# Old-state contributions of three groups placed inside the weight unit that stood ahead of them

## The chip, the cores and the metric

The kernel runs on one core of one Trainium2 chip. The metric is the device time in microseconds (us) of one execution; lower is better. Engines are named as in the profile: PE (TensorE), with PEld for its weight loads, DVE (VectorE), ACT (ScalarE), POOL (GpSimd) and SP (SyncE).

## The reference

One layer of a streaming encoder on 512 prompt rows and 8 streams of 16 sampled rows, in fp32. Between two half-step feed-forward blocks stands a mixer with a gated linear recurrence (branch A) and a state-space branch (branch B). The change lies in branch B, in how the sampled rows use the state that they start from:

```python
x = x + 0.5 * _swiglu(_rmsnorm(x), ffn1)
proj = _rmsnorm(x) @ w_in               # lru_x | lru_gate | z | xBC | dt | gate logits
xbc  = silu(causal_conv(xbc))           # xs, B, C; four groups of eight heads
states = concat([h0, chunk states])     # h0: the old state of each stream
y_off  = einsum('bclgn,bcgepn,bcgel->bclgep', C, states_in, exp(A_cs))
y = y_diag + y_off + D * xs;  final state is an output too
m = g_lru * (y_lru @ w_br_lru) + g_ssd * (rmsnorm(y * silu(z)) @ w_br_ssd)
x = x + m @ w_out
x = x + 0.5 * _swiglu(_rmsnorm(x), ffn2)
```

For the sampled rows `states_in` is `h0`, so their part of `y_off` is C times the old state: the "contributions" below.

## The kernel before

Features lie on the 128 partitions and the 640 tokens (512 + 128) along the rows. Every weight matrix is taken in units of 1024 x 128 numbers (8 tiles of 128 x 128). SP loads a unit into `w_raw`, ACT rounds it to `w_hi` (L977), DVE subtracts to get `w_lo` (L1343), and PE multiplies, for each of 8 tiles k, `w_hi` and `w_lo` with `act_hi` and `w_hi` with `act_lo`, each in two halves of 320 tokens: 48 matmuls (L635), summed in a PSUM buffer. There are two such buffers, `pu0` and `pu1`, used in turn by all "outs": each unit's result, and also the results of `old_states` and `new_states` below. PE opens an out only when DVE has freed the one two before it (`out_free`, in `open_out`). ACT begins the weight cut for the unit after next when a unit's result is ready (`take`).

The order of the work is written out by hand, the same on each engine. Branch B goes through four groups g; in each, after five steps of the chunked scan, the sampled streams' part is done on PE in this order: a unit, `old_states(0)` (16 transposes of the first half of the old states, L879; DVE copies them to `h0_t`, L1786), `inner` (L840), the units named in `middle`, `from_states(0)` (16 contributions `h0_t` x C, 128 x 16 each, L889, into `pn0`; the profile has two matmul records and two weight loads for each), `old_states(1)`, `new_states(0)` (L901), `from_states(1)`, `new_states(1)`, and then the next units. `h0_t` holds one half of the old states only.

`middle` holds one unit in groups 0, 1 and 2 (one of the next group's B and C columns, "xb") and none in group 3. What the others do with its result sets when its PSUM buffer is free: ACT takes its cut (L977), copies the result to `ext` (L1079 to L1082), DVE does three convolution taps (L1337) and frees the buffer after the first. DVE's own order there is: sums of squares (L1358), the three taps, then the copies of `old_states(1)` (L1786). ACT squares (L988) just ahead of the cut. `xf`, `es`, `h0_a` and `h0_b` are rows, decays and old states of the group (the profile writes `h_t`, `h_a`, `h_b`).

Of the kernel before, what the change touches and what calls it, by code (L numbers as in the profile page):

```python
# [17 lines left out]
P = 128  # L18
D_MODEL = 1024
SEQ, DEC_B, DEC_L = 512, 8, 16  # L20
TOK = SEQ + DEC_B * DEC_L
HALF = TOK // 2
KT = D_MODEL // P
# [72 lines left out]
U_AT, O_AT = {}, {}  # L96
# [67 lines left out]
def layer(nc, x_prompt, x_sample, state_lru_conv, state_lru_h, state_ssd_conv, state_ssd_h,  # L164
# [7 lines left out]
    with ctx:  # L172
        def sb(stack, name, shape, dt=F32):
            return stack.enter_context(nc.sbuf_tensor(name, shape, dt))

        s = {n: ctx.enter_context(nc.semaphore(n)) for n in SEMAPHORES}
# [8 lines left out]
        act_hi = sb(ctx, "act_hi", [P, KT, TOK], F32R)  # L185
        act_lo = sb(ctx, "act_lo", [P, KT, TOK], F32R)
# [81 lines left out]
        with ExitStack() as sc:  # L268
# [12 lines left out]
            h0_t = sb(sc, "h0_t", [P, 2, DEC_B, NS])  # L281
# [7 lines left out]
        pn = [ctx.enter_context(nc.psum_tensor(f"pn{i}", [P, 2, 512], F32)) for i in range(2)]  # L289
# [9 lines left out]
        def xft(g, k):  # L299

            return xf[:, k, :] if k < PAIRS else bc[:, g % 2, k - PAIRS, :]
# [10 lines left out]
        def out(o):  # L312

            return pu[o % 2][:, :, 0:HALF]
# [19 lines left out]
        def _(sp):  # L334
# [14 lines left out]
            def load_ffn(u, o, ci, w_up, w_down, first):  # L349
                tile0 = 0  # L350
                for gi, n, uu, _, _, ud, _ in ffn_plan(u, o, ci):
                    with sp.Fori(1 if first and gi == 0 else 0, n) as i:
                        for k in range(2):
                            load(k, uu, 2, i, cols(w_up, i * P + (tile0 * P + k * FFN)))
                    with sp.Fori(0, KT // 2) as i:
                        for k in range(2):
                            load(k, ud, 2, i, cols(w_down, i * (2 * P) + k * P, tile0, n), n)
                    tile0 += n
# [260 lines left out]
        def _(pe):  # L619
            def open_out(o):  # L620

                if not (isinstance(o, int) and o < 2):
                    pe.wait_ge(s["out_free"], o - 1)

            def products(dst, side, tiles, hi, lo, ready=None):

                n, at, ins = 3 * len(tiles), 0, None
                for k, c in tiles:  # L630
                    for w, a in ((w_hi, hi), (w_lo, hi), (w_hi, lo)):
                        if ready and w is w_hi and k >= ready[3]:
                            pe.wait_ge(s[ready[0 if a is hi else 1]], ready[2] + (k + 1))
                        for h in range(2):
                            ins = pe.matmul(dst[:, h, :], w[:, side, c, :], a[:, k, h * HALF:(h + 1) * HALF],  # L635
                                            start=(at == 0), stop=(at == n - 1))
                        at += 1
                ins.then_inc(s["out_ready"], 1)

            def unit(ub, ob, per_u, per_o, i, hi, lo, nk=KT, ready=None):  # L640

                pe.wait_ge(s["w_lo_done"], i * per_u + (ub + 1))
                open_out(i * per_o + ob)
                products(out(ob), ub % 2, [(t, t) for t in range(nk)], hi, lo, ready)

            def norm_sum(sq_end):

# [68 lines left out]
            for t in range(NT):  # L716
                pe.wait_ge(s[f"xin{t}"], 16)
                open_out(t)
                for k in range(KT):
                    ins = pe.transpose(pu[t % 2][:, k // 4, (k % 4) * P:(k % 4 + 1) * P],  # L720
                                       x_rows[:, t, k * P:(k + 1) * P], ident[:, :])
# [23 lines left out]
            for t in range(NT):  # L745
                ins = pe.transpose(pn[1][:, 0, t * HEADS:(t + 1) * HEADS], dt_raw[:, t * P:(t + 1) * P], ident[0:HEADS, 0:HEADS])
# [8 lines left out]
            for t in range(NT):  # L755
                pe.matmul(pn[1][:, 0, t * HEADS:(t + 1) * HEADS], gt_mask[:, t // (NT - 1), :], da_col[:, t, :],
                          start=True, stop=True)
            for t in range(NT):
                pe.matmul(pn[1][:, 1, (NT + t) * HEADS:(NT + t + 1) * HEADS], le_mask[:, t // (NT - 1), :], da_col[:, t, :],
                          start=True, stop=True)  # L760
            pe.matmul(pn[1][:, 1, 0:(NT - 1) * HEADS], ones[:, :],
                      da_col[:, 0:NT - 1, :].rearrange("p t h -> p (t h)"),
                      start=True, stop=True).then_inc(s["dt_p"], 1)
# [5 lines left out]
            for t in range(NT):  # L769
                ins = pe.transpose(pn[0][0:HEADS, t // 4, (t % 4) * P:(t % 4 + 1) * P], e_col[:, t, :], ident[:, :])  # L770
# [4 lines left out]
            with pe.Fori(4, KT) as j:  # L775
                lru_pair(j)

            def mix_unit(name, hi, lo, ready=None):
                unit(U_AT[name], O_AT[name], 0, 0, 0, hi, lo, ready=ready)

            def branch_unit(g, r):

                u, o = U_AT["br", g, r], O_AT["br", g, r]
                pe.wait_ge(s["w_lo_done"], u + 1)
                for m in range(2):
                    open_out(o + m)
                    products(out(o + m), u % 2, [(k, 2 * k + m) for k in range(PAIRS)], yn_hi, yn_lo,
                             ready=("yn_hi_done", "yn_lo_done", g * PAIRS, 0) if r == 0 and m == 0 else None)

            def lru_branch_unit(m):  # L790
                mix_unit(("bl", m), yl_hi, yl_lo, ("yl_hi_done", "yl_lo_done", 0, 0) if m == 0 else None)

            def fill(names):
                for name in names:
                    if name[0] == "br":
                        branch_unit(*name[1:])
                    elif name[0] == "bl":
                        lru_branch_unit(*name[1:])
                    else:
                        mix_unit(name, act_hi, act_lo)  # L800

            fill([("gl", 0), ("xb", 0, 4), ("xb", 0, 5)])
            for g in range(GROUPS):
# [31 lines left out]
                def inner(t):  # L835

                    sv(t, SV_G)
                    for h in range(HPG):
                        r = HD * (h % 2)
                        ins = pe.matmul(pn[0][r:r + HD, 0, (h // 2) * P:(h // 2 + 1) * P], xd[:, h, :], lmat[:, h, :],  # L840
                                        start=True, stop=True)
                    ins.then_inc(s["ssd_p"], 1)

                before, beside, behind, sampled_unit, middle, after = FILL[g]
                for k in range(PAIRS):
                    mix_unit(("xb", g, k), act_hi, act_lo)
                    if g and k == NORM_AT - 1:
                        norm_sum(SQ_GRP + g * SQG)
                fill(before)

                for t in range(NT - 1):
# [5 lines left out]
                    for q in range(PAIRS):  # L857
                        ins = pe.matmul(pn[0][:, 1, q * P:(q + 1) * P],  # L858
                                        ht[:, 2 * q:2 * q + 2, :].rearrange("n a b -> n (a b)"),
                                        xft(g, 5)[:, t * P:(t + 1) * P], start=True, stop=True)  # L860
                    ins.then_inc(s["ssd_p"], 1)
                    pe.matmul(pn[1][:, 1, :], b_tok[:, :], xdd[:, :, :].rearrange("p h d -> p (h d)"),  # L862
                              start=True, stop=True).then_inc(s["ssd_p"], 1)
# [3 lines left out]
                for q in range(PAIRS):  # L867
                    ins = pe.transpose(pn[1][:, 1, q * P:(q + 1) * P],
                                       ht[:, 2 * q:2 * q + 2, :].rearrange("n a b -> n (a b)"), ident[:, :])
                ins.then_inc(s["hp_mm"], 1)  # L870

                def old_states(qq):

                    pe.wait_ge(s[f"h0_in{qq}"], g * 32 + 32)
                    for a in range(2):
                        o = O_AT["old", g, qq] + a
                        open_out(o)
                        for b in range(DEC_B):
                            ins = pe.transpose(pu[o % 2][:, b // 4, (b % 4) * P:(b % 4 + 1) * P], h0[qq][:, a, b, :], ident[:, :])  # L879
                        ins.then_inc(s["out_ready"], 1)  # L880

                def from_states(qq):

                    for a in range(2):
                        q = 2 * qq + a
                        pe.wait_ge(s["out_free"], O_AT["old", g, qq] + a + 1)
                        for b in range(DEC_B):
                            c = SEQ + b * DEC_L
                            ins = pe.matmul(pn[0][:, 1, q * P + b * DEC_L:q * P + (b + 1) * DEC_L], h0_t[:, a, b, :],  # L889
                                            xft(g, 5)[:, c:c + DEC_L], start=True, stop=True)  # L890
                    return ins

                def new_states(qq):

# [12 lines left out]
                fill(sampled_unit)  # L907
                old_states(0)
                inner(NT - 1)
                fill(middle)  # L910
                from_states(0)
                old_states(1)
                pe.wait_ge(s["bseq"], g + 1)
                new_states(0)
# [13 lines left out]
            for a in range(TAIL_OUTS):  # L928
# [3 lines left out]
                for b in range(8):  # L932
                    ins = pe.transpose(pn[a % 2][0:rows, b // 4, (b % 4) * P:(b % 4 + 1) * P],
                                       src[:, 8 * (a % 4) + b, :], ident[:, :])
                ins.then_inc(s["tail_mm"], 1)
            with pe.Fori(0, KT // 2) as i:
                for k in range(2):
                    unit(U_OUT + k, O_OUT + k, 2, 2, i, act_hi, act_lo,
                         ready=("mh_done", "ml_done", 0, 0) if k == 0 else None)
            ffn(U_FFN2, O_FFN2, 22, h_hi, h_lo, act_hi, act_lo, XH_FFN2, last_sum, lambda: None)  # L940

            def to_rows(t, k):
                return pe.matmul(fin_at[t][:, k // 4, (k % 4) * P:(k % 4 + 1) * P], resid[:, k, t * P:(t + 1) * P], g_fin[:, k, :],
                                 start=True, stop=True)
# [9 lines left out]
            for k in range(KT):  # L954
                ins = to_rows(2, k)
            ins.then_inc(s["out_ready"], 1)
            pe.wait_ge(s["sq_added"], SQ_FIN + KT)
            for t in range(NT):
                ins = pe.matmul(pn[0][:, 0, t:t + 1], rvar[:, t * P:(t + 1) * P], ones[:, 0:1], start=True, stop=True)
            ins.then_inc(s["sq_summed"], 1)  # L960
            pe.wait_ge(s["y_a"], 1)
            for k in range(KT):
                ins = to_rows(3, k)
            ins.then_inc(s["out_ready"], 1)
            pe.wait_ge(s["y_v"], 1)
            for k in range(KT):
                ins = to_rows(4, k)
# [982 lines left out]
```

## Time and profile before

| | |
|---|---|
| median of 3 runs | 1974.1 us (1973.32 to 1975.79) |
| profiled execution | 1978.57 us |
| its span | 1977.0 us |
| PE busy | 1918.2 us, 97% of the span |
| DVE busy | 1078.0 us, 55% |
| ACT busy | 725.0 us, 37% |
| mean granted PE clock | 0.974 of full |

The span runs from the first to the last instruction that the profiler saw; the execution's own time is a little more. A busy PE isn't PE at its peak: matmuls are pipelined, and its clock has two levels, full (2.4 GHz) and half (1.2 GHz). The "granted clock" of a stretch is the mean over it, 1.00 at full and 0.50 at half.

### The profile page before, as it was taken

To read this page: it belongs to the slowest core of one execution; us is meant where nothing else is said; L and a number is where in the kernel's file an instruction comes from. 1 tells how busy PE (TensorE), PEld (TensorE's weight loads), DVE (VectorE), ACT (ScalarE), POOL (GpSimd) and SP (SyncE) were. 2 spreads that over 40 slices of the span, in tenths; PEclk is the share of its full clock that TensorE was granted. 3 is DMA by queue.
4 is the path that set the end of the run, shared out by engine and by line. 5 is a ranking of instruction groups with operands and counts; after the bars stand their busy time and mean duration, and the time that the engine had idled before them with its cause. 6 is when DMAs were issued, how large, how long until landed. Compare 5 with 4: busy or idle time off the path is not lost.

```text
span 1977.0 us, 31917 instructions
## 1 busy us (share of the span) xinstructions
PE 1918.2 (97%) x12877; PEld 1859.4 (94%) x12877; DVE 1078.0 (55%) x1355; ACT 725.0 (37%) x1141; POOL 113.0 (6%) x219
## 2 busy tenths in 40 slices
PE   8999999998899999999999999998799999999998
PEld 7999999998799999989998998987799999999998
DVE  6442443345687654566577677666745433442444
ACT  5221332223477644334545444542333221221222
POOL 2000000000012100001011010100000000000000
PEclk9999999999899999999998998997899999999999
DMA  4222222222222242334224323322622222222222
GB/s 140 74 70 75 68 83 73 76 67 84 91 72 74 72 119 86 95 98 124 78 70 113 103 78 111 96 69 78 224 76 65 74 75 76 74 76 76 75 66 77
DMA packets 268066, 171.68 MB, mean 87 GB/s; under 512 B 6534, under 2 KB 259642, under 8 KB 267677
## 3 DMA queue, kind: packets, MB, share of 16 engines
q1 hardware_dynamic: 239840, 129.52, 22.8%
q0 software_dynamic: 7072, 26.34, 4.3%
q10 hardware_dynamic: 21072, 14.69, 2.3%
q8 instruction: 57, 0.93, 0.2%
q14 instruction: 25, 0.20, 0.0%
HBM read 150.03 MB, written 20.48 MB: 86 GB/s over the span
## 4 chain that ended last, share of the span: by engine, by line
PE 85%; DVE 7%; ACT 3%; issue 2%; DMA 1%; DVEq 0%; ACTq 0%
PE pu L635 76%; PE pu L901 1%; DMA merged<-gate_spill 1%; PE pn L830 1%; PE pn L889 1%; ACT w_hi L977 1%; PE pn L858 1%; PE pn L840 1%; DVE h_t L1786 1%; PE pn L862 1%; DVE w_lo L1343 1%; DVE bc L1337 1%; DVE squares L1337 1%; PE pu L692 0%; DVE h_a L1793 0%
## 5 line engine op out<-in xcount | busy, mean ns | idle before, releaser
L1343 DVE TENSOR_TENSOR w_lo<-w_raw,w_hi 128x1024 fp32r<-128x1024 f32 x240 | 295.7, 1232 | 503.1 <-ACT w_hi L977 501.2
L635 PE MATMUL pu<-act_hi,w_hi 128*128 128x320 f32 x2336 | 542.3, 313 | 12.2 <-ACT act_hi L1004 7.4
L635 PE MATMUL pu<-act_lo,w_hi 128*128 128x320 f32 x2336 | 534.8, 310 | 2.1 <-DVE act_lo L1384 2.0
L635 PE MATMUL pu<-act_hi,w_lo 128*128 128x320 f32 x2336 | 534.0, 310 | 0.0
L977 ACT ACTIVATE w_hi<-w_raw 128x1024 fp32r<-128x1024 f32 x240 | 253.6, 1057 | 536.6 <-PE pu L635 532.9
L635 PEld LDWEIGHTS pu<-act_hi,w_hi 128*128 128x128 f32 x2336 | 394.4, 189 | 28.0 <-issue 21.0
L635 PEld LDWEIGHTS pu<-act_lo,w_hi 128*128 128x128 f32 x2336 | 391.9, 189 | 3.5 <-DVE act_lo L1384 3.1
L635 PEld LDWEIGHTS pu<-act_hi,w_lo 128*128 128x128 f32 x2336 | 392.8, 189 | 0.0
L635 PE MATMUL pu<-h_hi,w_hi 128*128 128x320 f32 x1056 | 241.7, 310 | 0.7 <-DVE ff_g L1401 0.7
L635 PE MATMUL pu<-h_lo,w_hi 128*128 128x320 f32 x1056 | 241.5, 310 | 0.0
L635 PE MATMUL pu<-h_hi,w_lo 128*128 128x320 f32 x1056 | 241.0, 309 | 0.0
L635 PEld LDWEIGHTS pu<-h_hi,w_hi 128*128 128x128 f32 x1056 | 177.4, 189 | 1.1 <-DVE ff_g L1401 0.9
L635 PEld LDWEIGHTS pu<-h_lo,w_hi 128*128 128x128 f32 x1056 | 177.4, 189 | 0.3 <-DVE h_lo L1410 0.3
L635 PEld LDWEIGHTS pu<-h_hi,w_lo 128*128 128x128 f32 x1056 | 177.3, 189 | 0.0
L635 PE MATMUL pu<-yn_hi,w_hi 128*128 128x320 f32 x256 | 63.7, 331 | 7.3 <-DVE acc_ssd L1663 5.3
L1012 ACT ACTIVATE ff_t<-ff_g 128x640 f32<-128x640 f32 x44 | 32.6, 740 | 92.5 <-DVE ff_g L1401 92.5
L635 PE MATMUL pu<-yn_lo,w_hi 128*128 128x320 f32 x256 | 59.8, 315 | 3.5 <-DVE yn_lo L1856 3.5
L1232 ACT ACTIVATE m_hi<-le_mask,da_hr 128x128 fp32r<-128x128 f32 x160 | 48.9, 390 | 29.5 <-PE pn L889 22.8
L635 PE MATMUL pu<-yn_hi,w_lo 128*128 128x320 f32 x256 | 59.3, 313 | 0.0
L635 PEld LDWEIGHTS pu<-yn_hi,w_hi 128*128 128x128 f32 x256 | 44.1, 193 | 12.8 <-DVE acc_ssd L1663 6.1
L1337 DVE SCALAR_TENSOR_TENSOR ff_a<-ff_t,ff_g 128x640 f32<-128x640 f32 x44 | 36.3, 826 | 35.4 <-ACT ff_t L1012 35.4
L1232 ACT ACTIVATE m_lo<-le_mask,da_lo 128x128 fp32r<-128x128 f32 x160 | 48.8, 388 | 0.0
(319 smaller groups left out, 1980.0 us busy)
## 6 DMA issues: line engine op xcount, KB each, us to landing
w_raw<-in_ffn_w_up_dram SPq DMA_DIRECT2D x87, 512.0 KB, 3.8
w_raw<-in_w_in_dram SPq DMA_DIRECT2D x73, 512.0 KB, 3.9
w_raw<-in_ffn_w_down_dram SPq DMA_DIRECT2D x32, 512.0 KB, 3.8
w_raw<-in_w_br_ssd_dram SPq DMA_DIRECT2D x16, 512.0 KB, 3.4
w_raw<-in_ffn_w_down_dram SPq DMA_DIRECT2D x16, 384.0 KB, 3.4
es<-e_spill POOLq DMA_DIRECT2D x40, 128.0 KB, 2.9
merged<-gate_spill POOLq DMA_DIRECT2D x8, 640.0 KB, 5.3
h_a<-in_state_ssd_h_dram POOLq DMA_DIRECT2D x8, 512.0 KB, 6.3
```

What stands on the lines that cost most here:

```text
L635: ins = pe.matmul(dst[:, h, :], w[:, side, c, :], a[:, k, h * HALF:(h + 1) * HALF], start=(at == 0), stop=(at == n - 1))
L830: ins = pe.matmul(pn[1][:, b, :], gt_r[:, t // (NT - 1), :], m[:, 4 * b:4 * b + 4, :].rearrange("p h l -> p (h l)"), start=(part == 0), st ...
L840: ins = pe.matmul(pn[0][r:r + HD, 0, (h // 2) * P:(h // 2 + 1) * P], xd[:, h, :], lmat[:, h, :], start=True, stop=True)
L858: ins = pe.matmul(pn[0][:, 1, q * P:(q + 1) * P], ht[:, 2 * q:2 * q + 2, :].rearrange("n a b -> n (a b)"), xft(g, 5)[:, t * P:(t + 1) * P] ...
L862: pe.matmul(pn[1][:, 1, :], b_tok[:, :], xdd[:, :, :].rearrange("p h d -> p (h d)"), start=True, stop=True).then_inc(s["ssd_p"], 1)
L889: ins = pe.matmul(pn[0][:, 1, q * P + b * DEC_L:q * P + (b + 1) * DEC_L], h0_t[:, a, b, :], xft(g, 5)[:, c:c + DEC_L], start=True, stop=True)
L901: ins = pe.matmul(pu[o % 2][:, b, :], xdd[rows, 2 * q:2 * q + 2, :].rearrange("p h d -> p (h d)"), b_seq[rows, :, :].rearrange("p b n -> p ...
L977: act.activation(w_hi[:, side, :, :], w_raw[:, side, :, :], ACT.Copy).then_inc(s["w_hi_done"], 1)
L1012: act.activation(ff_t[:, :], ff_g[:, :], ACT.Tanh, scale=0.5).then_inc(s["ff_th"], 1)
L1232: ins = act.activation(dst[:, h, :], le_mask[:, t // (NT - 1), :], ACT.Copy, scale=col)
L1337: return dve.scalar_tensor_tensor(out=dst, in0=a, scalar=scalar, in1=b, op0=op0, op1=op1)
L1343: dve.tensor_tensor(w_lo[:, side, :, :], w_raw[:, side, :, :], w_hi[:, side, :, :].bitcast(F32), ALU.subtract).then_inc(s["w_lo_done"], 1)
```

## The change

In groups 0, 1 and 2 the middle unit takes functions to be called amid its tiles: after tile k = 2 the eight contributions of the first part of `from_states(0)`, after tile k = 5 those of the second part. Before, both followed the unit. Group 3 has no middle unit and keeps its order. No wait is added or dropped: each part waits for its copy (`out_free`) as before.

```diff
@@ -622,7 +622,7 @@
                 if not (isinstance(o, int) and o < 2):
                     pe.wait_ge(s["out_free"], o - 1)
 
-            def products(dst, side, tiles, hi, lo, ready=None):
+            def products(dst, side, tiles, hi, lo, ready=None, amid=None):
 
 
 
@@ -635,13 +635,15 @@
                             ins = pe.matmul(dst[:, h, :], w[:, side, c, :], a[:, k, h * HALF:(h + 1) * HALF],
                                             start=(at == 0), stop=(at == n - 1))
                         at += 1
+                    if amid and k in amid:
+                        amid[k]()
                 ins.then_inc(s["out_ready"], 1)
 
-            def unit(ub, ob, per_u, per_o, i, hi, lo, nk=KT, ready=None):
+            def unit(ub, ob, per_u, per_o, i, hi, lo, nk=KT, ready=None, amid=None):
 
                 pe.wait_ge(s["w_lo_done"], i * per_u + (ub + 1))
                 open_out(i * per_o + ob)
-                products(out(ob), ub % 2, [(t, t) for t in range(nk)], hi, lo, ready)
+                products(out(ob), ub % 2, [(t, t) for t in range(nk)], hi, lo, ready, amid)
 
             def norm_sum(sq_end):
 
@@ -775,8 +777,8 @@
             with pe.Fori(4, KT) as j:
                 lru_pair(j)
 
-            def mix_unit(name, hi, lo, ready=None):
-                unit(U_AT[name], O_AT[name], 0, 0, 0, hi, lo, ready=ready)
+            def mix_unit(name, hi, lo, ready=None, amid=None):
+                unit(U_AT[name], O_AT[name], 0, 0, 0, hi, lo, ready=ready, amid=amid)
 
             def branch_unit(g, r):
 
@@ -879,16 +881,20 @@
                             ins = pe.transpose(pu[o % 2][:, b // 4, (b % 4) * P:(b % 4 + 1) * P], h0[qq][:, a, b, :], ident[:, :])
                         ins.then_inc(s["out_ready"], 1)
 
+                def from_state(qq, a):
+
+                    q = 2 * qq + a
+                    pe.wait_ge(s["out_free"], O_AT["old", g, qq] + a + 1)
+                    for b in range(DEC_B):
+                        c = SEQ + b * DEC_L
+                        ins = pe.matmul(pn[0][:, 1, q * P + b * DEC_L:q * P + (b + 1) * DEC_L], h0_t[:, a, b, :],
+                                        xft(g, 5)[:, c:c + DEC_L], start=True, stop=True)
+                    return ins
+
                 def from_states(qq):
 
-                    for a in range(2):
-                        q = 2 * qq + a
-                        pe.wait_ge(s["out_free"], O_AT["old", g, qq] + a + 1)
-                        for b in range(DEC_B):
-                            c = SEQ + b * DEC_L
-                            ins = pe.matmul(pn[0][:, 1, q * P + b * DEC_L:q * P + (b + 1) * DEC_L], h0_t[:, a, b, :],
-                                            xft(g, 5)[:, c:c + DEC_L], start=True, stop=True)
-                    return ins
+                    from_state(qq, 0)
+                    return from_state(qq, 1)
 
                 def new_states(qq):
 
@@ -907,8 +913,10 @@
                 fill(sampled_unit)
                 old_states(0)
                 inner(NT - 1)
-                fill(middle)
-                from_states(0)
+                if middle:
+                    mix_unit(middle[0], act_hi, act_lo, amid={2: lambda: from_state(0, 0), 5: lambda: from_state(0, 1)})
+                else:
+                    from_states(0)
                 old_states(1)
                 pe.wait_ge(s["bseq"], g + 1)
                 new_states(0)
```

On PE, in group 0, inside the middle unit: the rows at the unit's third and fourth tile (`pu0` is the unit's PSUM buffer, `act_hi` and `act_lo` the two parts of the activations, `w_hi` and `w_lo` of the weights). Before:

```order
L635 MATMUL pu0<-act_hi,w_hi 128x320 x2
L635 MATMUL pu0<-act_hi,w_lo 128x320 x2
L635 MATMUL pu0<-act_lo,w_hi 128x320 x2
L635 MATMUL pu0<-act_hi,w_hi 128x320 x2
L635 MATMUL pu0<-act_hi,w_lo 128x320 x2
L635 MATMUL pu0<-act_lo,w_hi 128x320 x2
```

In the changed kernel the first eight contributions (`pn0<-bc,h0_t`) stand between the two tiles:

```order
L635 MATMUL pu0<-act_hi,w_hi 128x320 x2
L635 MATMUL pu0<-act_hi,w_lo 128x320 x2
L635 MATMUL pu0<-act_lo,w_hi 128x320 x2
L890 MATMUL pn0<-bc,h0_t 128x16 [waits out_free]
L890 MATMUL pn0<-bc,h0_t 128x16 x7
L635 MATMUL pu0<-act_hi,w_hi 128x320 x2
L635 MATMUL pu0<-act_hi,w_lo 128x320 x2
L635 MATMUL pu0<-act_lo,w_hi 128x320 x2
```

At the unit's end, on PE in the same group, the rows from the last tile to the transposes of the second half of the old states (`h0_b`). Before:

```order
L635 MATMUL pu0<-act_hi,w_hi 128x320 x2
L635 MATMUL pu0<-act_hi,w_lo 128x320 x2
L635 MATMUL pu0<-act_lo,w_hi 128x320 x2
L889 MATMUL pn0<-bc,h0_t 128x16 [waits out_free]
L889 MATMUL pn0<-bc,h0_t 128x16 x7
L889 MATMUL pn0<-bc,h0_t 128x16 [waits out_free]
L889 MATMUL pn0<-bc,h0_t 128x16 x7
L879 MATMUL pu1<-ident,h0_b 128x128 [waits out_free,h0_in1]
L879 MATMUL pu1<-ident,h0_b 128x128 x7
L879 MATMUL pu0<-ident,h0_b 128x128 [waits out_free]
L879 MATMUL pu0<-ident,h0_b 128x128 x7
```

In the changed kernel:

```order
L635 MATMUL pu0<-act_hi,w_hi 128x320 x2
L635 MATMUL pu0<-act_hi,w_lo 128x320 x2
L635 MATMUL pu0<-act_lo,w_hi 128x320 x2
L881 MATMUL pu1<-ident,h0_b 128x128 [waits out_free,h0_in1]
L881 MATMUL pu1<-ident,h0_b 128x128 x7
L881 MATMUL pu0<-ident,h0_b 128x128 [waits out_free]
L881 MATMUL pu0<-ident,h0_b 128x128 x7
```

The transposes follow the unit's last matmul directly; what waits for what is the same as before, and the other engines' orders are unchanged.

## Rows read from the trace of the kernel before

**Rows 1.** The page: busy time of each engine, its share of the span, instructions.
```profile
PE 1918.2 (97%) x12877; PEld 1859.4 (94%) x12877; DVE 1078.0 (55%) x1355; ACT 725.0 (37%) x1141; POOL 113.0 (6%) x219
```

**Rows 2.** Timeline of group 0: start and length in us, engine, line, operation, [idle before].
```profile
830.25 2.17 PE L879 MATMUL pu<-ident,h_a 128*128 128x128 f32 x16
...
830.58 1.06 ACT L977 ACTIVATE w_hi<-w_raw 128x1024 fp32r<-128x1024 f32 x1 [4.56 <-PE pu L635]
...
832.81 2.35 DVE L1786 COPY h_t<-pu 128x1024 f32<-128x1024 f32 x2
...
834.18 0.53 PE L635 MATMUL pu<-act_hi,w_hi 128*128 128x320 f32 x2 [0.74 <-DVE h_t L1786]
...
840.55 2.94 DVE L1358 TENSOR_TENSOR rvar<-rvar,squares 128x512 f32<-128x512 f32 x4
...
841.30 3.64 PE L889 MATMUL pn<-bc,h_t 128*128 128x16 f32 x32
841.34 1.36 ACT L988 ACTIVATE squares<-xf 128x512 f32<-128x512 f32 x2 [2.04 <-DVE rvar L1358]
842.60 1.04 ACT L977 ACTIVATE w_hi<-w_raw 128x1024 fp32r<-128x1024 f32 x1
...
846.26 1.57 PEld L879 LDWEIGHTS pu<-ident,h_b 128*128 128x128 f32 x8 [0.32 <-DVE bc L1337]
847.96 2.35 DVE L1786 COPY h_t<-pu 128x1024 f32<-128x1024 f32 x2
...
849.33 2.17 PE L901 MATMUL pu<-b_seq,xdd 64*128 64x512 f32 x8 [1.10 <-DVE h_t L1786]
...
851.42 3.74 PE L889 MATMUL pn<-bc,h_t 128*128 128x16 f32 x32
...
855.10 3.47 PE L901 MATMUL pu<-b_seq,xdd 64*128 64x512 f32 x8
...
858.50 0.72 PE L635 MATMUL pu<-act_hi,w_hi 128*128 128x320 f32 x2
```

**Rows 3.** PE in stretches: bounds, length, busy time (instructions), granted clock, DMA share, GB/s.
```profile
834.18:841.30 7.12, 7.12 (x49) 1.00 0.26 72
...
844.78:848.25 3.47, 3.45 (x18) 0.56 0.61 149
...
1033.51:1037.58 4.07, 4.07 (x35) 0.85 0.00 0
...
1041.53:1044.26 2.73, 2.73 (x9) 0.70 0.02 6
1044.26:1049.08 4.82, 4.82 (x34) 0.74 0.69 200
1049.08:1052.80 3.72, 3.72 (x10) 0.50 0.09 25
1192.71:1196.20 3.49, 3.49 (x35) 1.00 0.00 0
...
1200.74:1204.07 3.33, 3.33 (x9) 0.57 0.00 0
1204.07:1208.33 4.26, 4.26 (x34) 0.85 0.75 220
1208.33:1212.05 3.72, 3.72 (x10) 0.50 0.11 30
...
1344.44:1351.23 6.79, 3.66 (x18) 0.50 0.00 0
1351.23:1354.94 3.71, 3.71 (x8) 0.50 0.02 4
1354.94:1361.88 6.94, 6.94 (x34) 0.50 0.51 151
1361.88:1365.60 3.72, 3.72 (x10) 0.50 0.00 0
```

**Rows 4.** The transposes of the old states (L879) of the second half, on PE: minimum, median, maximum ns.
```profile
L879 PE MATMUL pu<-ident,h_b x64: 272/421/476, 844.8 to 1347.7; 128*128 128x128 f32 x64
```

## The prediction

> **What bounds the kernel now.** I read the page first: TensorE (PE) is busy for 1918.2 us, 97% of the span, VectorE (DVE) for 55% [rows 1]. So time is lost only where PE waits, or where it runs at the lower of its two clock levels. The change touches one place, three times: the end of each of groups 0, 1 and 2. I then read the timeline of that place in group 0 [rows 2]; groups 1 and 2 repeat its pattern. Last I cut the same place of all four groups into stretches by what PE does, and read the granted clock of each [rows 3].
>
> What the reader is to see in group 0: The middle weight unit (L635) starts on PE at 834.18. At 841.30 PE goes on to the first 16 old-state contributions ("pieces" from here on: 32 short matmul records, L889), and at 844.78 to the transposes of the second half of the old states (L879). While the pieces run, the others deal with the unit's result: ScalarE (ACT) starts its weight cut at 842.60, then copies the result out, and DVE convolves it. Only when DVE's first tap has freed that PSUM buffer may PE do the second eight transposes (their weight loads start at 846.26). Then DVE finishes the taps, copies the transposed states (847.96), and only this copy lets PE start the new states (L901, 849.33). So from the unit's end to 849.33 the end is set by ACT and DVE, not by PE: the 3.48 us of pieces are work that PE does for nothing, under cover of a wait.
>
> **The change part by part.** Nothing is added or removed: 16 contributions (32 matmul records) in each of three groups move from behind the unit into it, eight behind its third tile and eight behind its sixth. There are no new semaphore increments and no DMA. Neither piece of eight waits: both copies that they need are DVE's 2.35 us from 832.81, over by 835.16 [rows 2], and the first piece would start three eighths into a unit of 7.12 us, 834.18 + 2.67 = 836.85. Switching between the forms costs nothing that I can see in a row; I take 0 (at most some 0.1 us a joint, two new joints a group, 0.6 us in all).
>
> What the move does is to make the unit end 3.48 us later, while the chain ACT cut, copy out, taps, state copy starts only at the unit's end. Before, the cut started 842.60 − 841.30 = 1.30 us behind the unit, since ACT was busy with squares until 842.70. At another unit, where ACT was idle, it started 830.58 − 830.25 = 0.33 us behind. So the later chain gets 0.97 us back and starts 3.48 + 0.33 − 1.30 = 2.51 us later than before [rows 2]. From the cut to the start of the new states it takes 849.33 − 842.60 = 6.73 us, none of it PE's own speed as long as the second transposes (start 846.26, 3.66 us behind the cut) end before the taps do.
>
> Now the new length of the place, counted from where the unit ends in the kernel before to where PE starts the next dense unit:
> 3.48 (pieces, now inside the unit) + 0.33 + 6.73 + first new states + second pieces + last new states.
> The last three depend on PE's clock, and here the rows give both levels. First new states: 851.42 − 849.33 = 2.09 at full clock, 3.71 in group 3 at half. Second pieces: 855.10 − 851.42 = 3.68 at full, 6.94 in group 3 at half. Last new states: 3.72 at half (groups 1 to 3), 2.09 at full [rows 2, 3]. So a group takes 18.40 us all at full clock and 24.91 us all at half.
>
> Before, it took 858.50 − 841.30 = 17.20, 1052.80 − 1033.51 = 19.29 and 1212.05 − 1192.71 = 19.34 us: 55.83 in the three [rows 2, 3].
>
> Which clock? The granted clock fell to half (1.2 GHz) behind every run of pieces in the kernel before: 0.56 in the transposes behind those of group 0, 0.85 already within those of group 1 [rows 3]. It came back to full (2.4 GHz) at once where PE then had full work, and late where it didn't: group 3, which has no middle unit, did its transposes and then idled (3.66 us busy in 6.79), and the clock stayed at 0.50 through 3.71, 6.94 and 3.72 us. Now look at what PE has after the change. Pieces of half the length between tiles of dense matmuls will probably no longer pull the clock down by themselves. But behind the unit there are then 0.33 + 6.73 = 7.06 us before the new states, with 16 transposes in them and else waiting. Group 0 needs 3.47 us for such 16 with most of the clock at half; at full each takes 272 ns instead of 421 [rows 4], so they are over sooner still. That is as little work as in group 3's stretch (3.66 us in 6.79). So I expect the clock to fall in that wait, after which the first new states run at half (3.71), the last ones too (3.72), and the second pieces lie between the rows of groups 1 and 2 (4.82, 4.26: the clock came back during the first new states and was lost again) and group 3's 6.94. I take the middle of 4.54 and 6.94, 5.74. A group: 3.48 + 7.06 + 3.71 + 5.74 + 3.72 = 23.71; three: 71.1; against 55.83: **+15.3 us**.
>
> The Trainium skill, page "TensorE: Matmul & The Clock Gate", section "Loop structure matters more than you think", speaks against this change in the same sense: matmuls that follow each other immediately stay warm, and a wait between bursts sends the array to half rate. Taken to its end, half rate from the wait onward, it gives the all-half case, which is the second rival below; group 3's 0.50 rows agree with it, the 1.00 of group 0's second pieces shows that short waits don't do it.
>
> Group 3 itself is not edited, but it will meet the clock in another phase of its work. Its second pieces ran wholly at half (6.94); in two of three other cases they cost about 4.5. It can hardly get worse: −2.4 × 2/3 = −1.6 us. Nothing else moves; the waits of PE behind this place are on DVE and ACT, which come as late as PE, so nothing swallows the delay. Sum: 15.3 − 1.6 = **+13.7 us**. The profiled execution took 1978.57 us (span 1977.0), 4.5 above the median of the runs shown, 1974.1; the sum is a difference, and I add it to the median: 1987.8.
>
> **The rivals.**
> 1. *The clock behaves as in group 0 now* (falls only for the last new states, 3.40 us there): 3.48 + 7.06 + 2.09 + 3.68 + 3.40 = 19.71 a group, 59.1 in all, +3.3 us, 1977.4. For it: two windows of full clock in group 0 in spite of a short wait. Against: the wait is now 5 us in two parts, not 1.1.
> 2. *All half*: 24.91 a group, +18.9 us, no help from group 3: 1993.0. If besides the pieces still pull the clock down within the unit, its last two tiles (a quarter of 7.12 us) may take twice as long, +1.8 us a group: 1998.
> 3. *The clock as in groups 1 and 2* (first new states 2.73 or 3.33, pieces 4.54, last 3.72): 21.83 a group, +9.7, 1983.8, or 1982 with group 3's gain. I count it with the forecast's own range.
> 4. *Faster, by the clock*: the short pieces hold the full level through the unit, and the waits are too short to lose it. Then 18.40 a group, 55.2 in three: −0.6 us, no change that can be told. It becomes faster only if group 3 also escapes: at full clock its two new-state blocks and pieces would save 1.62 + 3.26 + 1.63 = 6.5 us, in all −7: 1967. It decides only if the granted clock stays 1.00 through the waits of all four groups; the 0.50 of group 3 speaks against it.
> 5. *The move hides itself*: the unit's result was not urgent, because DVE is late anyway. Then +0: 1974. Against: the transposes waited for DVE's taps [rows 2], and DVE's sums of squares are over by 840.55 + 2.94 = 843.49 in either order.
>
> **How the numbers follow.** Chances: the forecast with case 3 (+8 to +17) 0.62; all half or worse 0.22; case 1 0.09; full clock or hidden, no change, 0.05; faster 0.02. What a measurement of this kernel can tell from no change is about 0.2%, 4 us. Case 1 lies just inside that, half of it goes to "same": slower 0.88, same 0.10, faster 0.02. The likeliest is 1987.8. The range leaves out part of the worst case above and case 1 and better below: 1979 to 1995.
>
> **What the changed profile would show.** Right: in groups 0 to 2 the unit's L635 matmuls span some 10.6 us with two blocks of pieces in it; ACT's cut starts about 0.3 us behind it; PE idles some 2.9 us before the second eight transposes, then about 2 us before the new states; granted clock 0.50 from that wait on, and second pieces over 4.2 us. Wrong: granted clock 1.00 there, ACT's cut later than 0.3 us behind the unit, or a stretch from the unit's start to the next dense unit of less than 7.12 + 20 us (nearer 18.40 than 23.71 behind the unit). What would make the forecast wrong is the clock: all of the spread between +3 and +19 hangs on it.

## The result: slower by 0.7%

The changed kernel takes 1987.62 us (median of 6, 1986.66 to 1991.53), the kernel before 1974.94 (median of 6, 1971.3 to 1976.34). The ratio is 1.0068, with a 95% interval of 1.0047 to 1.0088. The profiled execution took 1991.53 us with a span of 1989.9, against 1978.57 and 1977.0. Both lie some 4 us above the median of their kernel, so in other executions single groups may have taken less than the profiles show.

The page of the changed kernel: busy time of each engine, as in [rows 1].

```profile
PE 1921.1 (97%) x12877; PEld 1859.9 (93%) x12877; DVE 1078.5 (54%) x1355; ACT 725.7 (36%) x1141; POOL 112.7 (6%) x219
```

PE's busy time grew by 2.9 us, with the same number of instructions, in a span longer by 12.9. Neither the page's totals nor its list of lines tells where; the place itself does. The timeline of group 0 in the changed kernel, which answers to [rows 2] (start and length in us, engine, line, operation, [idle before]; contributions are now L890, transposes L881, ACT's cut L985, taps L1345, copies L1794, new states L907):

```profile
833.87 0.53 PE L635 MATMUL pu<-act_hi,w_hi 128*128 128x320 f32 x2 [0.74 <-DVE h_t L1794]
...
836.59 1.85 PE L890 MATMUL pn<-bc,h_t 128*128 128x16 f32 x16
...
841.01 1.85 PE L890 MATMUL pn<-bc,h_t 128*128 128x16 f32 x16
841.03 1.36 ACT L996 ACTIVATE squares<-xf 128x512 f32<-128x512 f32 x2 [2.03 <-DVE rvar L1366]
...
844.55 1.04 PE L881 MATMUL pu<-ident,h_b 128*128 128x128 f32 x8
...
844.75 1.06 ACT L985 ACTIVATE w_hi<-w_raw 128x1024 fp32r<-128x1024 f32 x1 [2.36 <-PE pu L635]
...
847.49 2.73 DVE L1345 SCALAR_TENSOR_TENSOR bc<-ext,vec,bc 128x640 f32<-128x640 f32 x3 [0.35 <-ACT bc L1090]
848.42 0.85 PEld L881 LDWEIGHTS pu<-ident,h_b 128*128 128x128 f32 x8 [3.08 <-DVE bc L1345]
848.43 1.09 PE L881 MATMUL pu<-ident,h_b 128*128 128x128 f32 x8 [2.84 <-DVE bc L1345]
...
850.13 2.35 DVE L1794 COPY h_t<-pu 128x1024 f32<-128x1024 f32 x2
...
851.49 3.78 PE L907 MATMUL pu<-b_seq,xdd 64*128 64x512 f32 x8 [1.97 <-DVE h_t L1794]
```

ACT had done its squares at 842.39 and stood idle for 2.36 us, until the unit had ended (844.55). The cut starts 0.20 us behind the unit, but that is 3.76 us behind where the unit used to end (833.87 + 7.12 = 840.99), against 1.30 before. PE waits twice: its weight loads stand 3.08 us and its matmuls 2.84 us for DVE's first tap, where the weight loads of [rows 2] stood 0.32 us and the matmuls had no gap; then its matmuls stand 1.97 us for DVE's copy, where [rows 2] had 1.10.

PE in stretches, as in [rows 3] (bounds, length, busy time, granted clock, DMA share, GB/s): group 0 first, then group 1 from the transposes on, group 2, and group 3, which the change does not touch.

```profile
833.87:840.99 7.12, 7.12 (x52) 1.00 0.26 73
840.99:844.55 3.56, 3.56 (x31) 1.00 0.00 0
844.55:848.43 3.88, 1.04 (x11) 1.00 0.06 6
848.43:851.49 3.06, 1.09 (x8) 0.80 0.59 164
851.49:855.21 3.72, 3.72 (x9) 0.50 0.00 0
855.21:862.14 6.93, 6.93 (x34) 0.50 0.54 154
862.14:865.86 3.72, 3.72 (x10) 0.50 0.00 0
1044.94:1051.88 6.94, 3.00 (x19) 0.74 0.29 76
1051.88:1055.37 3.49, 3.49 (x8) 0.54 0.02 5
1055.37:1059.48 4.11, 4.11 (x34) 0.88 0.79 226
1059.48:1063.20 3.72, 3.72 (x10) 0.50 0.12 34
...
1214.31:1218.03 3.72, 3.72 (x9) 0.50 0.00 0
1218.03:1224.96 6.93, 6.93 (x34) 0.50 0.53 151
1224.96:1228.68 3.72, 3.72 (x10) 0.50 0.00 0
...
1372.56:1376.44 3.88, 3.88 (x34) 0.94 0.85 242
```

The clock is at full through the unit with its two blocks of contributions, in all three groups (10.68 us at 1.00 in groups 1 and 2 too). In group 0 it is still 1.00 through the first wait, 0.80 over the second transposes and the second wait, and 0.50 from the new states on. In groups 0 and 2 everything from the new states to the next dense unit runs at half. (A dense unit is a weight unit: 48 matmuls of 320 columns, one behind the other.)

### The profile page after: what moved, and what is told of

The parts are those of the page before. It is cut to its first block, busy times and chain, and to the rows that moved or that the text cites. A ratio compares the mean times of both kernels' runs of the same rounds, so it can differ in the third digit from the quotient of the medians.

```text
span 1989.9 us, 31917 instructions
## 1 busy us (share of the span) xinstructions
PE 1921.1 (97%) x12877; PEld 1859.9 (93%) x12877; DVE 1078.5 (54%) x1355; ACT 725.7 (36%) x1141; POOL 112.7 (6%) x219
## 4 chain that ended last, share of the span: by engine, by line
PE 87%; DVE 6%; ACT 3%; issue 2%; DMA 1%; DVEq 0%; ACTq 0%
PE pu L635 77%; PE pn L890 2%; PE pu L907 1%; PE pn L832 1%; DMA merged<-gate_spill 1%; PE pn L860 1%; PE pn L842 1%; ACT w_hi L985 1%; PE pn L864 1%; DVE w_lo L1351 1%; DVE bc L1345 1%; DVE h_t L1794 1%; DVE squares L1345 1%; DVE xc L1345 0%; PE pn L652 0%
## 5 line engine op out<-in xcount | busy, mean ns | idle before, releaser
L985 ACT ACTIVATE w_hi<-w_raw 128x1024 fp32r<-128x1024 f32 x240 | 253.7, 1057 | 544.5 <-PE pu L635 541.4
L1345 DVE SCALAR_TENSOR_TENSOR ff_a<-ff_t,ff_g 128x640 f32<-128x640 f32 x44 | 36.3, 826 | 35.5 <-ACT ff_t L1020 35.5
```

What stands on the lines that cost most here:

```text
L985: act.activation(w_hi[:, side, :, :], w_raw[:, side, :, :], ACT.Copy).then_inc(s["w_hi_done"], 1)
L1345: return dve.scalar_tensor_tensor(out=dst, in0=a, scalar=scalar, in1=b, op0=op0, op1=op1)
```

## The experiments

For each kernel I read two lengths in its profile, group by group, from the timeline of PE. Both count from the start of the middle unit plus 7.12 us, which is where the whole unit used to end (in group 3, from the start of its first contributions): to the start of the first new states, and to the start of the next dense unit. Kernels are named by what they do; all were timed beside the kernel before.

| kernel | median us (before) | ratio, 95% interval | to the new states, groups 0, 1, 2 | to the next unit, groups 0, 1, 2, 3 |
|---|---|---|---|---|
| before | 1974.94 | | 8.03, 8.02, 8.02 | 17.20, 19.29, 19.34, 25.17 |
| changed | 1987.62 (1974.94) | 1.0068, 1.0047 to 1.0088 | 10.50, 10.50, 10.50 | 24.87, 21.82, 24.87, 21.95 |
| half inside | 1983.0 (1974.08) | 1.0039, 1.0023 to 1.0055 | 8.73, 8.71, 8.72 | 23.10, 21.89, 20.03, 25.17 |
| early tiles | 1990.95 (1974.08) | 1.0085, 1.0069 to 1.0101 | 13.63, 15.21, 10.50 | 24.72, 26.45, 21.83, 25.17 |
| late cut | 1989.3 (1974.08) | 1.0078, 1.0061 to 1.0095 | 10.33, 10.33, 10.33 | 21.50, 24.70, 21.68, 23.98 |
| filled waits | 1979.56 (1974.08) | 1.0022, 1.0008 to 1.0036 | 10.50, 10.50, 10.50 | 19.60, 21.23, 19.59, 22.12 |
| spread first | 1975.24 (1974.44) | 0.9998, 0.9988 to 1.0008 | 8.03, 8.03, 8.02 | 18.46, 17.62, 17.95, 25.17 |
| spread both | 1968.89 (1974.44) | 0.9970, 0.9959 to 0.9980 | 8.03, 8.03, 8.02 | 16.61, 16.61, 16.62, 22.01 |
| spread all | 1963.53 (1974.44) | 0.9938, 0.9922 to 0.9954 | 8.02, 8.02, 8.02 | 16.60, 16.60, 16.60, 19.38 |
| second only | 1971.75 (1974.44) | 0.9986, 0.9975 to 0.9997 | 8.03, 8.02, 8.02 | 18.04, 17.14, 17.26, 25.98 |
| changed, clock kept | 1970.45 (1974.34) | 0.9978, 0.9967 to 0.9988 | 10.52, 10.51, 10.51 | 19.09, 19.09, 19.08, 19.38 |

Within a kernel the column for the new states agrees to 0.02 us, but for "early tiles", where the clock fell within the unit: it is the chain on ACT and DVE. The last column scatters for one and the same order of work, by up to 4.6 us between the groups of a kernel and by 3.2 us in group 3 where it is not edited: it is the clock. It is read from one execution of each kernel, the ratio from all of them.

**Half inside.** The second eight contributions stand behind the eighth and last tile, so the unit ends before them.

```diff
-amid={2: lambda: from_state(0, 0), 5: lambda: from_state(0, 1)}
+amid={2: lambda: from_state(0, 0), 7: lambda: from_state(0, 1)}
```

> Only the first eight contributions stay inside the middle unit (behind its third tile); the second eight follow its last matmul, as before. My theory (the unit's result comes later by the time of the pieces inside it, and DVE's state copies with it): the unit ends 1.8 us later instead of 3.6, the weight cut, held until 1.30 us behind the old end by squares, starts some 0.8 us later, the first new states too, and the place of three groups costs 2 to 9 us more than in the kernel before: about +5, 1980. Rival (what costs is the cutting up of the unit, by joints or by the clock inside it): half the joints, half the cost of the full change, +6.5, and the new states start no later than in the kernel before.

The new states start 8.72 us behind the unit's old end, 0.70 later than before. The unit had grown by 1.78 us, so 1.08 of them were free: ACT is at its squares in that time. The rival's "no later than before" is out. The time rose by 0.39%, some 8 us, within the 2 to 9 expected but above the 5 in the middle, and more than 3 × 0.7 us explain; the rest is half clock, from the first new states on in group 0 (3.71, 6.94 and 3.72 us).

**Early tiles.**

```diff
-amid={2: lambda: from_state(0, 0), 5: lambda: from_state(0, 1)}
+amid={0: lambda: from_state(0, 0), 1: lambda: from_state(0, 1)}
```

> Both parts inside the unit, but behind its first and second tile instead of the third and sixth. My theory: only the unit's end counts, which is the same, so the time is that of the changed kernel, +12.5 within 3 us. Rival (the places inside the unit matter, because two blocks close together pull the clock down within the unit): the last six tiles run partly at half clock, up to 3.4 us more a group, up to +23 in all.

The granted clock in the unit, from its start to behind the second block, and over its last six tiles, in groups 0, 1 and 2:

```profile
831.89:838.14 6.25, 6.25 (x44) 0.84 0.31 82
838.14:845.70 7.56, 7.56 (x37) 0.68 0.00 0
1031.47:1039.12 7.65, 7.65 (x44) 0.68 0.24 66
1039.12:1046.86 7.74, 7.74 (x37) 0.66 0.00 0
1197.58:1202.89 5.31, 5.31 (x44) 1.00 0.35 98
1202.89:1208.26 5.37, 5.37 (x39) 1.00 0.00 0
```

The rival's mechanism is there: two blocks only one tile apart pulled the clock down within the unit in two groups of three, and six tiles took 7.6 and 7.7 us instead of 5.37. What failed in my expectation is that the unit would end as in the changed kernel. That its end sets the new states holds: they start 6.94 us behind it in all three groups (852.64 − 845.70 in group 0), as in the changed kernel (851.49 − 844.55). The total is 16.9 us above the kernel before, just outside my 12.5 within 3, and far from the rival's 23; against the changed kernel it is about 3 us more, and the two intervals overlap. A later end of 3.1 us in group 0 cost nothing in all (24.72 us against 24.87), as the clock came back sooner behind it.

**Late cut.** The order on PE is that of the kernel before; ACT gets three copies, whose result nobody uses, ahead of the middle unit's cut (the line that adds the semaphore `pad` is left out).

```diff
+                if middle:
+                    act.wait_ge(s["xb_out"], XB_AT[middle[0]])
+                    for r in range(3):
+                        act.activation(rtmp[:, :], act_hi[:, r, :].bitcast(F32), ACT.Copy).then_inc(s["pad"], 1)
+                        act.wait_ge(s["pad"], 3 * g + r + 1)
                 fill(middle)
```

> The order of the kernel before on PE, contributions behind the unit; added are three copies of 640 columns on ACT (into a scratch row that is free) ahead of the middle unit's weight cut in groups 0 to 2, some 2.5 us, so that the cut starts as late against PE's work as in the changed kernel. My theory: PE loses the same as in the changed kernel without any edit of its own order, since the new states start 2.5 us later and the clock falls in the wait: +8 to +19, about +13. Rival (the move on PE costs by itself, the chain behind the unit has slack): within 3 us of the kernel before.

Its timeline in group 0:

```profile
839.35 3.64 PE L889 MATMUL pn<-bc,h_t 128*128 128x16 f32 x32
...
842.93 1.06 ACT L977 ACTIVATE w_hi<-w_raw 128x1024 fp32r<-128x1024 f32 x1
...
846.61 1.97 PE L879 MATMUL pu<-ident,h_b 128*128 128x128 f32 x8 [2.54 <-DVE bc L1342]
...
849.68 3.79 PE L901 MATMUL pu<-b_seq,xdd 64*128 64x512 f32 x8 [1.10 <-DVE h_t L1791]
```

The cut starts 3.58 us behind the unit, the new states 10.33. No matmul of PE stands elsewhere in its order, and the kernel loses 0.78%, as much as the change. This is the sharpest test of the chain: the delay of ACT's cut is enough, and the rival "the chain has slack" is out.

**Filled waits.** The changed kernel with dense matmuls whose result nobody uses in PE's two waits: 18 ahead of the second eight transposes, 12 ahead of the new states.

```diff
+                def dense(n):
+                    for _ in range(n):
+                        for h in range(2):
+                            pe.matmul(pn[1][:, h, 0:HALF], gt_r[:, 0, :], act_hi[:, 0, h * HALF:(h + 1) * HALF],
+                                      start=True, stop=True)
...
+                        if qq == 1 and a == 1 and middle:
+                            dense(9)
...
+                if middle:
+                    dense(6)
```

> The changed kernel with 18 matmuls of 320 columns (result unused) on PE ahead of the second eight transposes and 12 ahead of the new states, in groups 0 to 2, so that PE works through its two waits; the chain on ACT and DVE is as late as in the changed kernel. My theory: the waits stay as long, but the granted clock stays 1.00 there; the group takes about 18.4 us instead of 23.9, that is 12 to 17 us less than the changed kernel and within 4 us of the kernel before. Rival (the cost is the wait alone, the clock little): within 3 us of the changed kernel, +12.7.

Its timeline in group 0, from the new states on:

```profile
852.57 2.17 PE L916 MATMUL pu<-b_seq,xdd 64*128 64x512 f32 x8 [0.21 <-DVE h_t L1805]
...
854.67 3.75 PE L899 MATMUL pn<-bc,h_t 128*128 128x16 f32 x32
...
858.34 1.99 PE L916 MATMUL pu<-b_seq,xdd 64*128 64x512 f32 x8
...
860.30 2.35 DVE L1822 TENSOR_TENSOR h_b<-h_b,pu 128x1024 f32<-128x1024 f32 x2
...
861.67 0.53 PE L635 MATMUL pu<-act_hi,w_hi 128*128 128x320 f32 x2 [1.34 <-DVE h_b L1822]
```

The new states start as late as in the changed kernel, and now run at full clock (2.10 us instead of 3.72). The rival ("the clock little") is out, but that gave back 8 to 9 us, not 12 to 17; it stands at +0.22%. The last row says why: at full clock PE comes to the next unit 1.34 us too early. DVE adds to `h_b` only after its outputs, which wait for the contributions, and so frees the buffer late. Half clock had hidden that wait. In group 1 the clock fell in the contributions once more (0.73 over them, 0.50 over the last new states; 21.23 us).

**Spread first, spread both, spread all, second only.** From the kernel before; quarters of the first contributions are put between dense matmuls and transposes (first part), the second contributions in halves around one of the last new states, which DVE adds ahead of its outputs (second part). The edit is shown shortened: calls that stand one to a line in the kernel are joined, and the splitting of the helpers is left out.

```diff
-                from_states(0)
-                old_states(1)
+                from_state(0, 0, 0, 4); dense(3); from_state(0, 0, 4, 8); dense(2)
+                from_state(0, 1, 0, 4); old_state(1, 0); dense(1)
+                from_state(0, 1, 4, 8); old_state(1, 1); dense(1 if middle else 10)
...
                 new_states(0)
-                from_states(1).then_inc(s["ssd_p"], 1)
-                new_states(1)
+                from_state(1, 0); new_state(1, 0); dense(2)
+                from_state(1, 1).then_inc(s["ssd_p"], 1); new_state(1, 1)
...
-                outputs(NT - 1, lambda: new_states(1))
+                new_states(1, (0,))                       # on DVE
+                outputs(NT - 1, lambda: new_states(1, (1,)))
```

"Spread first" has the first part in groups 0 to 2, "spread both" both parts there, "spread all" both in all four groups, "second only" the second part in all four.

> Kernel before, unit whole, in groups 0 to 2: behind the unit the contributions go in quarters between dense matmuls (3 and 2 pairs of 320 columns whose result is unused) and between the two halves of the second transposes, all inside the wait that PE has there (new states not before 8.03 us behind the unit). Theory (the new states' start is set by ACT and DVE; the rest of a group's length is PE's clock): the new states start at 8.0 us in every group and run at full clock, 2.1 us instead of 2.7 and 3.3 in groups 1 and 2, the second contributions as before; a group takes 17.2 to 18.5 us, together 52 to 55 against 55.8: 0 to -4 us. Rival (PE's work behind the unit isn't covered, so that the added matmuls cost what they take): 3 x 1.8 us, +5.

> The last one, and behind the first new states the other contributions in two halves, with half of the last new states and 2 unused dense pairs between them; DVE adds that half ahead of its outputs, so that the next unit's buffer comes free earlier. Theory: the clock is kept to the end, and the next unit starts 16.5 us behind the middle unit's end: 49.5 us in three groups against 55.8, -6 us. Rival (what is gained behind the new states is lost again, since the contributions end 1.6 us later and ACT and DVE wait for them): 0 to -2 us.

> The same in group 3 too, which has no middle unit: there 10 unused dense pairs fill PE's wait for the state copies. Group 3's place took 25.2 us at half clock; theory at full: 10.8 to the new states + 2.1 + 1.84 + 1.05 + 0.6 + 1.84 + 1.05, 19.3 us: -6 more, -12 in all, 1962. Rival (the half clock of group 3 costs nothing, since DVE is the bound there): as the last one, -6.

> Only the second half of the last change, in all four groups (other contributions in two halves around half of the last new states, 2 unused dense pairs, DVE adds that half first); the first contributions whole behind the unit, as in the kernel before. Theory: the next unit no longer waits for DVE behind the contributions, and about half of the clock losses of the last new states (1.6 us each) go: -2 to -5 us. Rival (no clock gain without the first part, as the clock is already down): -1 to +2.

The timeline of "spread all" in group 0, from the second transposes on:

```profile
847.51 1.07 PE L890 MATMUL pu<-ident,h_b 128*128 128x128 f32 x8
848.34 0.54 PE L876 MATMUL pn<-act_hi,gt_r 128*128 128x320 f32 x2
849.47 2.17 PE L921 MATMUL pu<-b_seq,xdd 64*128 64x512 f32 x8 [0.59 <-DVE h_t L1825]
851.57 1.96 PE L905 MATMUL pn<-bc,h_t 128*128 128x16 f32 x16
853.45 1.13 PE L921 MATMUL pu<-b_seq,xdd 64*128 64x512 f32 x4
854.51 0.86 PE L876 MATMUL pn<-act_hi,gt_r 128*128 128x320 f32 x4
855.21 1.85 PE L905 MATMUL pn<-bc,h_t 128*128 128x16 f32 x16
856.99 1.13 PE L921 MATMUL pu<-b_seq,xdd 64*128 64x512 f32 x4
858.05 0.56 PE L635 MATMUL pu<-act_hi,w_hi 128*128 128x320 f32 x2
```

All is at full clock, and the next unit starts 16.60 us behind the unit's end in each of three groups, where 16.5 was expected. The first part alone brought nothing that can be told (a ratio of 1.00 within 0.12%): it made the new states run in 2.10 us in every group, and the last ones lost the clock again (0.50 in group 0). The rival's 5 us for the added matmuls are out. The second part alone brought 0.14%, some 3 us as expected, though its interval (0.6 to 4.9 us) touches the rival's; both brought 0.30%, where the rival had 0.1% at most, and both with group 3 0.62%: 1963.53 us, faster than both kernels, with more work on PE than either. In group 3 the new states start 10.80 us behind the first contributions in both, and what follows took 25.17 − 19.38 = 5.8 us less, at 1.00 where the kernel before had 0.50.

**Changed, clock kept.** "Spread all" with the contributions of groups 0 to 2 inside the unit again, and 18 and 12 unused matmuls in the waits. The edit is shown against "spread all", shortened.

```diff
-                fill(middle)
-                from_state(0, 0, 0, 4); dense(3); ...
+                if middle:
+                    mix_unit(middle[0], act_hi, act_lo, amid={2: lambda: from_state(0, 0), 5: lambda: from_state(0, 1)})
+                    old_state(1, 0); dense(9); old_state(1, 1); dense(6)
+                else:
+                    from_state(0, 0, 0, 4); dense(3); ...
```

> The change under test (contributions inside the unit) together with everything that keeps the clock and frees the next unit's buffer early: 18 and 12 unused matmuls in the two waits of groups 0 to 2, the last new states and contributions interleaved with DVE's addition moved ahead, and group 3 filled, exactly as in the version with both parts spread in all groups. The two differ by where the first contributions stand, at a granted clock of 1.00 in both, so the difference is the late chain alone. Theory: new states 10.5 us behind the unit's old end instead of 8.03, a group 19.1 us instead of 16.6, and 3 x 2.5 = 7.4 us more than that version in all: about 1971, ratio 0.9975. Rival (the change costs mostly clock, the chain itself has slack once PE is at full clock): within 2 us of that version, 0.994.

1970.45 us, ratio 0.9978: 6.9 us above "spread all" by the medians and 7.9 by the ratios, give or take some 4, where 7.4 were expected and the rival had under 2. A group took 19.09 us where it had taken 16.60 (in group 0, 858.42 − 839.33), and group 3 the same 19.38 in both. The granted clock is 1.00 over all four groups in both, so this is the price of the late chain by itself: 3 × 2.49 = 7.5 us.

## Why the prediction was right

**The chain.** It said: the cut 0.33 us behind the unit, new states 10.54 us behind its old end. Measured: 0.20 and 10.50, in all three groups; the unit grew by 3.56 us (844.55 − 840.99), not 3.48, so the joints cost next to nothing. That the delay of ACT's cut does it is shown by "late cut", and its price of about 7 us alone by "changed, clock kept". In the changed kernel the later start is 3 × 2.47 = 7.4 us of the 15.7 that the three groups grew by; the other 8.3 came behind it, in the same work at a lower clock.

**The clock.** It said: full through the unit, lost in the wait, first and last new states at half. Measured: 1.00 in the unit, then 3.72, 3.49 and 3.72 us (said: 3.71) and three times 3.72. That it is the wait that loses the clock is shown by "filled waits". It was lost a little later than the prediction's sign said: in group 0 the first wait was still at 1.00, and 0.50 began with the new states. The second contributions, the most uncertain term, were set at 5.74; they took 6.93, 4.11 and 6.93, mean 5.99. The groups took 24.87 + 21.82 + 24.87 = 71.56 us, against 71.1. So the middle value was met by two groups in the all-half case and one in the case of groups 1 and 2 before; no group took the predicted 23.71. Which of the two a group falls into I could not foretell, and another execution may draw otherwise.

**Group 3.** It said −1.6 us; it took 21.95 instead of 25.17, −3.2: its second contributions ran at 0.94 instead of 0.50. Sum by the profiles: 71.56 − 55.83 − 3.2 = +12.5, the spans differ by 12.9, the medians by 12.7; the forecast was +13.7. The median forecast, 1987.8, met 1987.62 more closely than this deserves, as the interval of the ratio alone is 8 us wide, and it was added to a median of 1974.1 that is now 1974.94.

**What was mis-sized.** The fourth rival's "18.40 us a group all at full clock" left out DVE: at full clock it is 19.6 ("filled waits"), since the next unit waits 1.34 us for the addition to `h_b`. So even a clock of 1.00 throughout would have made the change slower, by 3 × 19.6 − 55.8 = 3 us in groups 0 to 2, not equal. And with group 3 at full clock too the same rival's −7 us would have been some −2 to −3: an estimate, as group 3 gave 5.8 us in "spread all", where DVE's addition was moved ahead, and would give less without. The rows that told it stood in the timeline before, DVE's work between the contributions (over at 855.10) and the next unit:

```profile
855.61 0.69 DVE L1740 TENSOR_TENSOR es<-es,pn 128x512 f32<-128x512 f32 x1
...
856.34 0.69 DVE L1742 TENSOR_TENSOR es<-es,pn 128x512 f32<-128x512 f32 x1
...
857.06 1.22 DVE L1803 TENSOR_TENSOR h_b<-h_b,pu 128x1024 f32<-128x1024 f32 x1
```

DVE's first addition to `h_b` ends at 858.28, 3.2 us behind the contributions, and the last new states take 2.1 at full clock. I had followed only the waits that were visible at the clock of that time. And in the second rival I had the clock fall within the unit only as an aside; with the blocks one tile apart it happened in two groups of three, three tiles apart in none.

## What to carry to other kernels

Short work on PE that stands in a wait is free where it is; moved ahead of a result on which another engine's chain depends, it costs its whole length less what that engine is late anyway (here 3.56 less about 1.1 us). Before moving such work, ask when the consumer would start at the earliest, not whether PE is busy 97% of the time. And where PE waits or does small matmuls, read the granted clock of what comes behind: filling the waits with dense matmuls whose result nobody uses, spreading the small ones between them, and freeing the buffer that then becomes the bound, turned a kernel of 1974.4 us into one of 1963.5.

## What the hardware showed that I had not expected

- Thirty-two matmuls of 16 columns took 3.68 us at full and 6.94 at half clock: they slow down at least as much as the eight matmuls of 512 columns of the new states (2.10 and 3.72). And the clock falls with no wait in sight: in group 1 of the kernel before it was 0.85 over 4.07 us in which PE was busy with them throughout [rows 3]. Sixteen of them, three tiles of dense matmuls (2.7 us), sixteen kept it at 1.00 in all three groups of the changed kernel; sixteen, one tile, sixteen did not in two groups of three (0.84 and 0.68, 0.68 and 0.66).
- Waits of 2.84 and 1.97 us on PE, with 1.04 and 1.09 us of transposes before and between them, cost the clock in all three groups; in groups 0 and 2 the half level then lasted over all the work up to the next dense unit, 14.37 us (851.49 to 865.86).
